# Records of all blocks fetched at once and kept in SBUF, and a gather that skips unused rows, in a mixture-of-experts layer

## The reference

```
scores = sigmoid(hf @ w_router)                 # 128 experts
eidx   = group-limited top 8 of scores + bias   # 8 groups of experts, the best 4 are allowed
wts    = scores[eidx] / sum * 2.5
# the 2048*8 (token, expert) pairs are sorted by expert and padded to blocks of 128 rows
row_tok = full(R, T);  row_w = zeros(R)         # padding: token T, weight 0
for each block of one expert e:
    xs = hp[row_tok]                            # hp: tokens of width 1024, a zero row at T
    y  = (silu(xs @ w_gate[e]) * (xs @ w_up[e])) @ w_down[e]      # inner width 256
    routed[row_tok] += y * row_w[:, None]
out = rmsnorm(x + gate2 * (routed + swiglu(hf, shared weights)))
```

## Time and profile before

| what | value |
|---|---|
| median of 3 runs | 3520.7 us (3518.12 to 3538.77) |
| span of the profiled execution | 3472.9 us |
| what lies around the span, against the median | 47.8 us |
| PE busy | 2951.9 us, 85% of the span |
| VectorE (DVE) busy | 2164.1 us, 62% |
| ScalarE (ACT) busy | 1706.3 us, 49% |
| GpSimd (POOL) busy | 925.5 us, 27% |
| moved by DMA | 730.08 MB, mean 210 GB/s |
| mean granted clock of TensorE | 0.935 |

### The profile page before, as it was taken

The page is one execution under the profiler, slowest core; times in us unless marked ns, Lnnn a source line. Parts: engine busy times, 40 slices in busy tenths (PEclk is TensorE's granted clock), DMA queues, the critical chain, the costliest instruction groups (busy, mean ns, idle before and its releaser), DMA issues.

```text
span 3472.9 us, 61999 instructions
## 1 busy us (share of the span) xinstructions
PE 2951.9 (85%) x13151; PEld 2180.6 (63%) x13152; DVE 2164.1 (62%) x3443; ACT 1706.3 (49%) x2435; POOL 925.5 (27%) x794
## 2 busy tenths in 40 slices
PE   6699999999469989888798888888888888998883
PEld 2355555555358877776676767676767667776662
DVE  1146666666643665667676766666766675667774
ACT  0133333333133654656565655556556565656565
POOL 0001111111223333232333333333332323333331
PEclk9899999999779999999899999999999999999896
DMA  9501111111175887989998999899989998899997
GB/s 368 163 25 49 49 48 36 49 36 43 67 182 122 239 228 208 269 260 259 289 295 252 290 281 274 258 271 285 288 259 265 265 293 232 247 266 280 294 275 249
DMA packets 415300, 730.08 MB, mean 210 GB/s; under 512 B 31521, under 2 KB 297377, under 8 KB 414754
## 3 DMA queue, kind: packets, MB, share of 16 engines
q1 hardware_dynamic: 341314, 500.17, 42.5%
q0 software_dynamic: 73824, 228.47, 28.6%
HBM read 587.37 MB, written 141.19 MB: 210 GB/s over the span
## 4 chain that ended last, share of the span: by engine, by line
DMA 45%; PE 22%; issue 12%; DVE 8%; POOL 7%; POOLq 4%; ACT 2%; DVEq 0%; SPq 0%; ACTq 0%
DMA rec<-rec_tab 42%; PE PB L986 8%; POOL arena L461 3%; POOL acc_tab L492 3%; POOLq L476 3%; PE PB L951 2%; PE PB L1068 2%; PE PB L1070 2%; PE PB L1069 2%; DMA arena<-in_ada_b 1%; PE PB L1045 1%; PE PB L956 1%; DMA acc_tab<-arena,rec 1%; PE PB L970 1%; PE PB L1011 1%
## 5 line engine op out<-in xcount | busy, mean ns | idle before, releaser
L887 DVE TENSOR_TENSOR WS<-RAW,WS (+1 forms) x774 | 900.8, 1219 | 127.3 <-ACT WS L586 125.3
L586 ACT CAST WS<-RAW (+1 forms) x774 | 759.5, 1052 | 153.2 <-DMA RAW<-in_w_up_e 99.6
L1068 PE MATMUL PB<-WS,XR 128*128 x1720 | 685.6, 399 | 52.2 <-issue 46.6
L461 POOL DMA_INDIRECT arena<-h_tab,rec x219 | 255.3, 1166 | 1574.7 <-DMA rec<-rec_tab 1381.1
L1070 PE MATMUL PB<-WS,XR 128*128 x1720 | 674.7, 392 | 0.0
L1069 PE MATMUL PB<-WS,XR 128*128 x1720 | 674.0, 392 | 0.0
L917 DVE SCALAR_TENSOR_TENSOR arena<-PB,rec,G 128x512 f32<-128x512 f32 x430 | 302.5, 745 | 383.7 <-DMA acc_tab<-arena,rec 336.5
L1068 PE MATMUL PB<-WS,HR 128*128 x860 | 402.9, 468 | 154.1 <-DVE HR L921 153.0
L492 POOL DMA_INDIRECT acc_tab<-arena,rec x215 | 402.5, 1872 | 93.3 <-issue 68.4
L1068 PEld LDWEIGHTS PB<-WS,XR 128*128 128x128 f32 x1720 | 327.6, 190 | 158.7 <-issue 91.8
L1069 PEld LDWEIGHTS PB<-WS,XR 128*128 128x128 f32 x1720 | 326.7, 190 | 66.1
(11 more groups left out here) (233 smaller groups left out, 2982.6 us busy)
## 6 DMA issues: line engine op xcount, KB each, us to landing
RAW<-in_w_gate_e SPq DMA_DIRECT2D x128, 1024.0 KB
RAW<-in_w_up_e SPq DMA_DIRECT2D x128, 1024.0 KB
RAW<-in_w_down_e SPq DMA_DIRECT2D x128, 1024.0 KB, 8.6
arena<-in_ada_w SPq DMA_DIRECT2D x12, 2048.0 KB, 14.3
arena<-in_x SPq DMA_DIRECT2D x32, 512.0 KB, 3.6
h_tab<-arena SPq DMA_DIRECT2D x17, 512.0 KB, 2.9
acc_tab<-arena SPq DMA_DIRECT2D x16, 512.0 KB, 2.6
out<-fa SPq DMA_DIRECT2D x16, 512.0 KB, 4.7
```

The costliest lines, as they stand in the source:

```text
L461: g.indirect_dma_start(xg[n % AHEAD], None, h2_tab, bass.IndirectOffsetOnAxis(ap=rec[:, n % UNROLL, 0:1], axis=0)).then_inc(s[f"xg_r{n % A ...
L586: nc.scalar.copy(to, of).then_inc(s["a_hig" if k < 4 else "a_hid"], 1)
L887: last = V.tensor_tensor(lo, raw, hi, ALU.subtract)
L1068: mm(bank, hi[:, k, :], w(k, 0), start=(k == 0), stop=False)
```

## The change

Blocks' records are no longer loaded one block at a time. After the tables are ready, GpSimd fetches the records of all 384 possible blocks with three indirect gathers (one block's 1 KB on each partition, `rec_rows`), PE transposes tokens and weights (six transposes into PSUM), and VectorE copies them to SBUF: `rec_i` (tokens, converted to integers) and `rec_w` (weights), column j for block j - 1. In the loop GpSimd copies one column of `rec_i` into a slot of `rec`, and VectorE reads its weight directly from `rec_w`. The token is stored as a float32 in the record instead of as an integer, and VectorE writes the padding instead of GpSimd. The gather gets a bounds check, so that indices of T and above transfer nothing; the four buffers `xg` are therefore set to zero once.

```
@@ gpsimd, setup
-            v = pad_rec.rearrange("p (a b c) -> p a b c", b=P, c=2)
-            g.iota(v[:, :, :, 0], pattern=[[0, T // P // 2], [1, P]], base=PAD, channel_multiplier=0).then_inc(s["z_rec"], 1)
-            g.memset(v[:, :, :, 1], 0).then_inc(s["z_rec"], 1)
-            g.iota(rec[:, :, 0], pattern=[[0, UNROLL]], base=PAD, channel_multiplier=1).then_inc(s["z_pool"], 1)
-            g.memset(rec[:, :, 1], 0).then_inc(s["z_pool"], 1)
...
-            g.wait_ge(s["z_pool"], 2)
-            for n in range(AHEAD + 2):
-                g.dma_start(rec[:, n, :], rec_tab[n * P:(n + 1) * P, :]).then_inc(s["rec_ld"], 16)
@@ gpsimd, ahead of the loop
-                g.indirect_dma_start(xg[n % AHEAD], None, h2_tab,
-                                     bass.IndirectOffsetOnAxis(ap=rec[:, n % UNROLL, 0:1], axis=0)).then_inc(s[f"xg_r{n % AHEAD}"], 16)
+                g.indirect_dma_start(xg[n % AHEAD], None, h2_tab, bass.IndirectOffsetOnAxis(ap=rec[:, n % UNROLL:n % UNROLL + 1], axis=0),
+                                     bounds_check=T - 1, oob_is_err=False).then_inc(s[f"xg_r{n % AHEAD}"], 16)
 
             g.wait_ge(s["e_off"], 1)
-            g.wait_ge(s["st_h2"], 16 + 16 * NT)
-            g.wait_ge(s["rec_ld"], 16 * (AHEAD + 2))
+            g.wait_ge(s["st_rec"], 16 * TOPK * NT)
+            for n in range(3):
+                g.indirect_dma_start(rec_rows[:, n, :], None, rec_tab.rearrange("(b t) a -> b (t a)", t=P),
+                                     bass.IndirectOffsetOnAxis(ap=offi[:, n:n + 1], axis=0)).then_inc(s["rec_got"], 16)
+            g.wait_ge(s["rec_go"], 2)
+            g.tensor_copy(rec[:, UNROLL - 1:UNROLL], rec_i[:, 0:1]).then_inc(s["rec_win"], 1)
+            g.tensor_copy(rec[:, 0:AHEAD + 1], rec_i[:, 1:AHEAD + 2]).then_inc(s["rec_win"], 1)
+            g.wait_ge(s["rec_win"], 2)
+            g.wait_ge(s["st_h2"], 16 * NT)
+            g.wait_ge(s["xg_z"], 1)
             for n in range(AHEAD):
                 gather(n)
@@ gpsimd, block b
-                            g.wait_ge(s["rec_ld"], b * 16 + 16 * (AHEAD + 2))
+                            g.wait_ge(s["rec_win"], b + 2)
                             gather(n + AHEAD)
                             g.wait_ge(s["y_v"], b + 2)
                             g.wait_ge(s["added"], b * 16 + 32)
                             settle(g)
                             (scatter-add of the block before, into acc_tab)
-                            load_rec(b + (AHEAD + 2), (n + AHEAD + 2) % UNROLL)
+                            k = (n + AHEAD + 1) % UNROLL
+                            g.tensor_copy(rec[:, k:k + 1], rec_i[:, bass.ds(b + (AHEAD + 2), 1)]).then_inc(s["rec_win"], 1)
@@ vector, setup
+            pads = pad_rec.rearrange("p (a b c) -> p a b c", b=P, c=2)
+            V.memset(pads[:, :, :, 1], 0.0).then_inc(s["z_rec"], 1)
+            v.wait_ge(s["c_cst"], 16)
+            V.tensor_scalar(pads[:, :, :, 0], C("iota").unsqueeze(1).to_broadcast([P, T // P // 2, P]), float(PAD), None, ALU.add).then_inc(s["z_rec"], 1)
@@ vector, after the tables
+            V.memset(arena[:, 36864:36864 + AHEAD * D], 0.0).then_inc(s["xg_z"], 1)
             V.memset(HR[:, :].bitcast(f32), 0.0).then_inc(s["hT_sb"], 1)
             v.wait_ge(s["hT_sb"], 1)
             v.sem_inc(s["y_v"], 1)
+            v.wait_ge(s["rec_tr"], 1)
+            V.tensor_copy(rec_i[:, :], B[4][:, 0:NENT]).then_inc(s["rec_go"], 1)
+            V.tensor_copy(rec_w[:, :], B[5][:, 0:NENT]).then_inc(s["rec_go"], 1)
+            v.wait_ge(s["rec_go"], 2)
             v.sem_inc(s["e_thr"], 1)
@@ vector, block b: the weight of the record
-    scalar=recf[:, (n - 1) % UNROLL, 1:2]
+    scalar=rec_w[:, bass.ds(b, 1)]
@@ tensor, after the tables
+            pe.wait_ge(s["rec_got"], 48)
+            for a in range(2):
+                for n in range(3):
+                    last = tr(B[4 + a][:, n * P:(n + 1) * P], rec_rows[:, n, :].rearrange("b (t a) -> b a t", a=2)[:, a, :], ident)
+            last.then_inc(s["rec_tr"], 1)
```

More of the change, by code:

```diff
@@ L36 @@
 NTABS = 10
+NENT = 3 * P
 GUW = 4096
@@ L124, in build @@
         acc_tab = nc.dram_tensor("acc_tab", [T + P, D], f32).ap()
-        rec_tab = nc.dram_tensor("rec_tab", [(E + 1) * T, 2], i32).ap()
+        rec_tab = nc.dram_tensor("rec_tab", [(E + 1) * T, 2], f32).ap()
         row_tab = nc.dram_tensor("row_tab", [NTABS * P], i32).ap()
@@ L204, in build @@
         gains = S[:, 1024:3072].rearrange("p (a n) -> p a n", a=2)
-        pad_rec = S[:, 3072:5120].bitcast(i32)
+        pad_rec = S[:, 3072:5120]
         zeros = S[:, 5120:6144]
@@ L221, in build @@
         recs = sb("recs", [P, TOPK, 2])
-        toki = sb("toki", [P, NT], i32)
         pos_i = sb("pos_i", [P, NT], i32)
@@ L227, in build @@
         nblk_i = sb("nblk_i", [1, 2], i32)
-        rec = sb("rec", [P, UNROLL, 2], i32)
-        recf = rec[:, :, :].bitcast(f32)
+        rec = sb("rec", [P, UNROLL], i32)
+        rec_i = arena[:, 47104:47104 + NENT].bitcast(i32)
+        rec_w = arena[:, 47104 + NENT:47104 + 2 * NENT]
         PB = ctx.enter_context(nc.psum_tensor("PB", [P, 8, 512], f32))
         B = [PB[:, n, :] for n in range(8)]
-        names = """c_wt c_cst c_pos c_ada0 c_ada1 c_ada2 c_win c_small c_vec c_rest settled z_pool z_fill z_rec z_dve
+        names = """c_wt c_cst c_pos c_ada0 c_ada1 c_ada2 c_win c_small c_vec c_rest settled z_fill z_rec z_dve
             p_mod p_xT p_sc p_rk p_proj p_bd p_h2T p_PT p_rt p_pv p_py p_qkT p_wo
@@ L295, in build @@
         FG = arena[:, 46080:47104]
+        rec_rows = arena[:, 43008:43776].rearrange("p (n a) -> p n a", n=3)
         fsq = arena[:, NT * D:NT * D + NT * D // 2].bitcast(bf16).rearrange("p (t n) -> p t n", t=NT)
@@ L328, in _ @@
             sp.wait_ge(s["c_cst"], 16)
-            sp.dma_start(rec_tab[0:T, :].rearrange("(p t) a -> p (t a)", p=P), C("shrec").bitcast(i32)).then_inc(s["z_fill"], 16)
+            sp.dma_start(rec_tab[0:T, :].rearrange("(p t) a -> p (t a)", p=P), C("shrec")).then_inc(s["z_fill"], 16)
             sp.wait_ge(s["z_dve"], 1)
@@ L473, in _ @@
             nblk = g.value_load(nblk_i[0:1, 0:1], min_val=NT + 1, max_val=NT + 255)
[L475 to L478, removed]
             with g.Fori(0, (256 + NT) // UNROLL) as q:
@@ L746, in step @@
                     V.tensor_copy(recs[:, :, 1], s8)
-                    tk = toki[:, bass.ds(i - 2, 1)] if not isinstance(i, int) else toki[:, i - 2:i - 1]
-                    V.tensor_copy(recs[:, :, 0].bitcast(i32), tk.to_broadcast([P, TOPK])).then_inc(s["v_recs"], 1)
+                    tk = C("tok")[:, bass.ds(i - 2, 1)] if not isinstance(i, int) else C("tok")[:, i - 2:i - 1]
+                    V.tensor_copy(recs[:, :, 0], tk.to_broadcast([P, TOPK])).then_inc(s["v_recs"], 1)
                 if ok(i + 1):
@@ L849, in _ @@
             V.tensor_scalar(s8[:, 0:3], gm[:, 0:3], 0.0, None, ALU.is_equal)
-            link(V.tensor_scalar(gneg[:, 0:3], gm[:, 0:3], float(P), None, ALU.mult))
-            link(V.scalar_tensor_tensor(out=gneg[:, 0:3], in0=gs[:, 0:3], scalar=float(T), in1=gneg[:, 0:3], op0=ALU.mult, op1=ALU.add))
-            V.tensor_scalar(offi[:, 0:3], gneg[:, 0:3], float((E + 1) * T - P), None, ALU.min)
+            link(V.tensor_copy(gneg[:, 0:3], gm[:, 0:3]))
+            link(V.scalar_tensor_tensor(out=gneg[:, 0:3], in0=gs[:, 0:3], scalar=float(T // P), in1=gneg[:, 0:3], op0=ALU.mult, op1=ALU.add))
+            V.tensor_scalar(offi[:, 0:3], gneg[:, 0:3], float((E + 1) * (T // P) - 1), None, ALU.min)
             link(V.tensor_scalar(eif[:, 0:3], m8[:, 0:3], 1.0, None, ALU.add))
@@ L916, in _ @@
                             for c in range(2):
-                                last = V.scalar_tensor_tensor(out=ys[(n - 1) % 2][:, c * 512:(c + 1) * 512], in0=B[4 + c], scalar=recf[:, (n - 1) % UNROLL, 1:2],
+                                last = V.scalar_tensor_tensor(out=ys[(n - 1) % 2][:, c * 512:(c + 1) * 512], in0=B[4 + c], scalar=rec_w[:, bass.ds(b, 1)],
                                                               in1=G2[:, c * 512:(c + 1) * 512], op0=ALU.mult, op1=ALU.mult)
```

14 lines of the change are left out of this document (5 added, 9 removed).

## The result

The changed kernel takes 3386.9 us (median of 4 runs, 3339.8 to 3399.6) beside 3519.4 for the one before on the same chip: ratio 0.954, 95% interval 0.943 to 0.964. On a second chip it was 3324.4 against 3496.1, ratio 0.951 (0.948 to 0.953). The profiled execution has a span of 3337.7 us, 135.2 less than before.

A forecast was written before the change was run, and what follows sets the result against it. Routed blocks were taken as held by GpSimd's wait on records, near-ceiling DMA load and VectorE's order. From 3520.7 us, minus 190 for the routed stretch, plus 2 for the way in: 3333 us, range 3280 to 3385 at 0.47.

The forecast's parts named there:

- The wait on the newest record load: GpSimd's gather waits for the record load just issued: turns of 11.8 us; at most VectorE's 336.5 us come back.
- the 420 us: Routed blocks' excess over a 9.3 us pace, shared by GpSimd's turn, DMA load and VectorE's order.
- The sum: Routed stretch: DMA work of 1969 us at a share of 0.94 gives 2095 us, a gain of 190.
- rival 1: Skipping padded rows saves no DMA time: routed gain 73 us, total 3450 us; chance 0.08.
- The scatter is late next: GpSimd's loop: the scatter's landing sets a turn of 9.3 to 10.1 us, bounding only runs of short blocks.
- The copy at 0.2 us: GpSimd's 128x1 copy replacing each block's record load: 0.2 us, free while the scatter is in flight.
- The skipped rows: Gathers in routed blocks: 8,960 pad rows, 36.7 MB, no longer read, worth 110 us of all engines.
- rival 3: Late weights take back the time in routed blocks: share stays 0.91, gain 121 us, total 3402 us; chance 0.10.
- The check from the blocks, 2000 us: Routed blocks at 9.3 or 11.3 us average 10.0, 2000 us, leaving 95 us for late weights.
- The way in: Between the table's store and the first block: extra record gathers, transposes and copies cost +2 us.
- The cover that I named: First block: ScalarE fetches transposes only from 981.84, behind its casts, hiding PE's delay; without it 5.5 us.
- The setup: Before the tiles: record pad moved to VectorE, six early record loads gone; costs nothing, 2 us if uncovered.

The follow-up runs named there:

- e5: Kernel before, records still loaded block by block, but each gather waits for its own record load instead of the newest: ratio 0.951, median 3371.6 us.
- e2: Changed kernel without the bounds check on the gather, so padded rows are read again: 3330.9 us, ratio 0.953 to the kernel before.
- e4: Changed kernel with the bounds check on the scatter-add too, so padded rows are not added: 3305.7 us, ratio 0.947 to the kernel before.
- e1: Changed kernel run again unaltered on a second chip: 3324.4 us, ratio 0.951 to the kernel before.
- e7: Changed kernel with an eighth of the bytes in each routed expert's weight load, so not the full layer: 3252.4 us, ratio 0.923 to the kernel before.
- e12: Kernel of e10 with gate and up weights loaded, awaited and released in two halves: 3321.1 us, ratio 0.943 to the kernel before.
- e11: Changed kernel with half the bytes in each routed expert's weight load, so not the full layer: 3274.5 us, ratio 0.929 to the kernel before.
- e10: Changed kernel with the skip in the scatter too, no zeroing, first four gathers issued early from constants: 3362.6 us, ratio 0.954 to the kernel before.

## Why the prediction was right, and where it was off

**The wait on the newest record load: right as the cause, much too low in the sum.** The prediction names it first of three things that share the 420 us, and e5 shows that relaxing it alone gives the whole gain. But "The sum" goes by DMA work over a share. With the bytes unchanged, which is rival 1's case, that gives the end of the wait only 73 us. Measured with the bytes unchanged, it is 133.0 us of routed stretch in e2 and 142.5 in e5.

**The scatter is late next, at a turn of 9.3 to 10.1 us, and bounds only in places: right.** It lands at 9.6, and VectorE's wait on it is 8.8 us.

**The copy at 0.2 us: too low, without effect.** It takes 0.75 us and 0.89 more until the gather, behind the scatter's landing.

**The skipped rows, priced at 110 us of all engines: the bytes right, their worth wrong.** This term, and "The sum" that divides DMA work by a share of 0.94, is the step that failed. 37 MB were forecast and 38.6 measured. In the sum they are worth 117 us (2079 instead of 1969, over 0.94). In the runs they are worth 6.5 us of the median (3330.9 - 3324.4, intervals overlap) and 13.6 to 22.6 us of routed stretch. The share did not stay where it was put, it followed the bytes: 0.94, 0.91 and 0.84 in e2, the changed kernel and e4, at 2135, 2112 and 2093 us. A busy share of 0.91 was no sign that the engines' total work was the bound.

**That the total came near is in large part luck.** The forecast gain of 190 us of routed stretch is 73 for the wait and 117 for the skip. The profiles give 133.0 for the wait (e2) and 22.6 more for the skip, together 156 (147 by e1). One term was too low by 60 and the other too high by 94. The second chip's medians give 172 us for the whole change, where 188 were forecast. Rival 1 had the skip's worth nearly right and its time of 3450 us wrong, since it priced the wait at 73. Of the signs that the prediction named, the idle time in front of the scatter, q0's bytes and VectorE's wait below 100 us came true. A share of 0.94, a block of 10.5 us, waits for weights of 150 us and first transposes at 978 to 980 did not: they are 0.91, 10.7, 116.2 (99.6 before), and 8.6 us later after the table's store than before. The share of 0.91 is rival 3's, but the waits that were to hold it there grew by only 17 us.

**The check from the blocks, 2000 us: near,** 1976 in e7. The remainder for late weights was put at 95 us and is 137 to 146, some 46 of them through PE's clock.

**The way in, +2 us: 5.2 us** (37.8 - 32.6). The record gathers were given 4.1 us to land; PE starts 10.0 us after the last one's issue, while SP's table store is in flight. The cover that I named doesn't hold: ScalarE's first casts run from 994.64 to 998.52, and it then waits 6.95 us for the transposes.

**The setup, nothing: right.** VectorE adds the last strip at 118.71 us, at 118.76 before.

**The tiles, +16.8 us in this profile, were not in the sum** and don't belong to the change: e1, the same kernel, ends them at 956.6. The forecast for the span is 3472.9 - 188 = 3285 us, and it measured 3337.7. Of these 53 us, 17 are the tiles, 34 the routed stretch and 3 the way in, less 1 in the shared stretch. The remainder of 47.8 us that the prediction adds to the span for the median is no cost outside it; on the first chip the changed kernel's median happened to lie 49.2 above its profile as well, on the second 1.0 below.

**Which rows of experts are late, and why, is only half settled.** e12 shows that handing the weights over earlier is worth 45.5 us with the same bytes. e11 has fewer bytes in all and shorter loads, and can't say which of the two counts. Which of landing, order of the queues or split is the largest part wasn't separated either. Two signs of slower weights point in opposite ways: ScalarE's waits for them rose from 99.6 to 116.2 us, while the down weights' median landing went from 8.6 us to 7.3 in e1. The packet rotation of the Trainium skill (DMA: Bandwidth & Descriptors, "Queues, rings and completion order") was not tested by any run.

## What to carry to other kernels

When a counted wait releases the first step of a turn, look up which transfer its number includes: a wait for all loads so far also waits for the newest, which nobody needs yet. Here, splitting the count over two semaphores gave what a rewrite of the data's path gave, 4.9% of the time. And don't price saved bytes by dividing the engines' work by a busy share; find who waits for the queue, since here, at a share near 0.9, 38 MB more or less changed the routed stretch by only 14 to 23 us of 2112.

## What the hardware showed that I hadn't expected

- The tiles, whose code all these kernels share but for the type of a copied token, ended between 956.6 and 1021.0 us in 14 profiles: within 3.1 us of each other for e1 to e4 on one chip, 993.5 to 1021.0 on the next two. This moves whole times by up to 2% and is probably the reason for the wide intervals. About half of it is PE at a lower granted clock: from 100 us to the table's store it is 0.90 in e5, e7 and e10, with PE busy for 751 to 757 us, and 0.92 to 0.93 in e1 and e4, with 727 to 732. Why the clock was lower there stays open.
- A 128x1 integer copy on GpSimd with an offset from a register takes 0.75 us (median of 215), where the same copy with a fixed offset ahead of the loop took 0.18.
- The bounds check lengthens a gather's issue from a median of 0.99 to 1.05 us, and the indices past the bound move no bytes (q0 207.95 to 169.81 MB in the routed stretch).
